# A hybrid attention and recurrence block on one core: where a recurrence head's keys and inputs are turned from feature-major to token-major

## The chip, the cores and the metric

The kernel runs on 1 core of one Trainium2 chip. The metric is the device time of one execution in microseconds (us), as the median of three runs. The engines are PE (TensorE; PEld is its weight loads), DVE (VectorE), ACT (ScalarE), POOL (GpSimd) and SP (SyncE, which only issues DMAs here).

## What is computed

The input x is 2048 x 1024 (f32). The block normalizes its rows, projects them with one matrix, and feeds two groups of heads: 8 attention heads over a sliding window of two chunks of 64 tokens, with a sink logit each, and 4 heads of a gated linear recurrence (HGRN2) of 128 features each. Both are gated with SiLU, joined, projected again, normalized and added to x. The recurrence is what the change touches, per head and chunk of 64 (the kernel works with chunks of 128, which it calls pairs):

```python
f = lb + (1 - lb) * sigmoid(f_logit); kk = 1 - f
G = cumsum(log(f))                      # inside a chunk
q_dec, k_dec = q * exp(G), kk * exp(-G)
A = tril(q_dec @ k_dec.T)
U = (kk * exp(G_last - G)).T @ v        # what the chunk adds to the state
state = exp(G_last) * state + U
o = A @ v + q_dec @ state_before
```

## The kernel before

The sequence is cut into 4 tiles of 512 tokens. All activations are kept with features on the partitions and tokens along the free dimension. A tile has 34 steps, one per block of weights: K (0), V (1), queries (2 to 5), attention gates (6 to 9), then four steps for each recurrence head h, `forget(h)`, `query(h)`, `value(h)` and `gate(h)` = 10 + 4h to 13 + 4h, and 8 steps of the output projection (26 to 33). In steps 0 to 25 PE runs 24 products L452 per step (8 slices of 128 features, each with high x high, low x high and high x low parts in FP32R); in the output steps it runs L461.

Everything else is placed into that stream by hand. `between` (L563) says ahead of which product of which step PE runs the small matmuls: `scores` and `turn` of the attention at product 4 of steps 8, 10, ..., 16, `weigh` at product 20, `head_scores(h)` at product 12 of step `gate(h)` (13, 17, 21, 25), `head_states(h)` at product 16 (head 0: 20) of the next step, `head_out(h)` at product 12 of step `gate(h) + 4` (head 3: product 16 of `gate(h) + 2`), `head_sum(h)` one step later. DVE and ACT each have one loop over tiles and steps (L1072 and L761), in which the order within a step is written out; the engines meet through counting semaphores.

A recurrence head goes like this. At `forget(h) + 1` DVE scales the logits out of PSUM (L1090), and ACT and DVE alternate through the logarithm of the gate and its cumulative sum (L1123 to L1160). At `query(h) + 1` DVE makes `k_mid` (L1137) and scales `f_d` (L1138). At `gate(h)`, which follows `value(h)`, DVE makes `q_mid` (L1108), `v_r`, the head's inputs (L1111), and `to_next` (L1112). `k_mid` and `v_r` are feature-major, but the state matmul (L540) and the output matmul (L549) need keys and inputs with tokens on the partitions. So `head_scores` waits for `k_mid` and `v_r` and turns both by 16 transposes on PE, each from 64 tokens' half of the partitions (L525), into the two banks of `score_b`; ACT copies them to `kv_tok` in one instruction (L810). Then PE computes the head's scores (L532). DVE masks them at the next step (`mask_head`, L1000). `head_states` waits for that mask and for `kv_tok`; `carry_head` (L1005 to L1020) chains the states on DVE.

`score_b` also holds the attention's scores (L481) and the sum of squares of a head's output (`head_sum`, L559), so PE waits in `head_scores` until DVE has read the attention's scores and ACT the previous sum, and in `scores` and ahead of the output steps until ACT has taken the turned keys.

Other work on the same queues at these steps: on DVE the softmax (`softmax_first` L1048 to L1057 at even steps from 8 to 14, `softmax_sums` L1062 to L1065 at odd steps from 9 to 15), the gating of the attention's output (L1129 at steps 11, 13, 15, 17), the gates' SiLU (L982, L986, L993 at step `gate(h) + 1`); in step 13 the order after `to_next` is softmax sums, then L1129, and PE's `turn` at step 14 (L493) waits for both. In tile 0 and the first six steps of tile 1, the weights are split into a high and a low part on the fly, ACT's L689 and then DVE's L906 at the end of nearly every step, for the block two or three steps on; SP saves them to memory, and later tiles load them ready-made. On ACT, the step `gate(h)` holds the eviction L810, then L689, then the squares of the previous head's output (L836, L837); POOL takes the low part of these (L1216) for `head_sum`.

## Time and profile before

| | before |
|---|---|
| median of 3 runs | 892.59 us (891.85 to 894.47) |
| profiled execution | 891.43 us |
| its span | 889.6 us |
| busy: PE, DVE, ACT, POOL | 877.8, 524.9, 422.1, 113.9 us |

The profiled execution lies 1.8 us above its span, which begins with the first instruction and ends with the last. A matmul's duration is its way through the array and overlaps its neighbours', so the pace of PE is read from the distance between starts. In a timeline row the columns are start, duration, engine, line, operation, output and input, shape and count; in brackets stands the idle time ahead of it and what ended that. A group `x8` of matmuls is merged into one row.

### The profile page before, as it was taken

What the parts mean: (1) busy time and instruction counts of PE and PEld (TensorE: products, weight loads), DVE (VectorE), ACT (ScalarE), POOL (GpSimd) and SP (SyncE); (2) the same over time, 40 slices, a digit from 0 to 9 for tenths busy, and PEclk for the clock granted to TensorE, in tenths of its full rate; (3) what the DMA queues carried; (4) which work ended last, traced back from release to release, by engine and by line L of the source; (5) the groups of instructions that cost most, each with busy time, mean ns of one, the idle gap of its engine ahead of it and who ended that gap; (6) DMA issues with size and microseconds to landing.
All of it is one profiled execution on the core that took longest, in us unless ns stands there. A gap on an engine that the chain in (4) does not pass through costs nothing.

```text
span 889.6 us, 12328 instructions
## 1 busy us (share of the span) xinstructions
PE 877.8 (99%) x4730; PEld 719.9 (81%) x4730; DVE 524.9 (59%) x848; ACT 422.1 (47%) x736; POOL 113.9 (13%) x90
## 2 busy tenths in 40 slices
PE   8999999999999999999999999999999999999997
PEld 6887788888888788888888877888888877788886
DVE  6778867763656764655153677465524367745523
ACT  7856456573654444445144534454523453445322
POOL 0000014420200001421020000242111000013012
PEclk9999999999999999999999999999999999999999
DMA  8686766629958543543785654345378544443463
GB/s 313 240 307 211 258 214 226 225 72 400 400 193 323 197 167 125 180 167 109 290 325 189 222 190 142 142 145 202 131 257 331 189 154 160 144 158 143 145 247 129
DMA packets 52922, 186.03 MB, mean 209 GB/s; under 512 B 5888, under 2 KB 6144, under 8 KB 52864
## 3 DMA queue, kind: packets, MB, share of 16 engines
q1 hardware_dynamic: 50128, 178.29, 56.3%
q10 hardware_dynamic: 2736, 6.95, 2.0%
q8 instruction: 38, 0.62, 0.3%
q14 instruction: 20, 0.16, 0.1%
HBM read 141.18 MB, written 44.04 MB: 208 GB/s over the span
## 4 chain that ended last, share of the span: by engine, by line
PE 95%; DVE 1%; ACT 1%; issue 1%; DMA 1%; SPq 0%; DVEq 0%; ACTq 0%
PE bank L452 62%; PE bank L461 10%; PE score_b L461 5%; PE turn_b L461 5%; PE bank L532 2%; PE turn_b L503 2%; PE score_b L481 2%; PE turn_b L549 2%; PE bank L540 2%; PE turn_b L552 2%; PE score_b L525 1%; PE turn_b L493 1%; DMA x_in<-in_x 1%; ACT w_hi L689 0%; PE score_b L560 0%
## 5 line engine op out<-in xcount | busy, mean ns | idle before, releaser
L452 PE MATMUL bank<-h_hi,w_hi 128*128 128x512 f32 x832 | 327.1, 394 | 1.3 <-ACT h_hi L726 1.3
L452 PE MATMUL bank<-h_hi,w_lo 128*128 128x512 f32 x832 | 327.5, 394 | 0.0
L452 PE MATMUL bank<-h_lo,w_hi 128*128 128x512 f32 x832 | 326.0, 392 | 0.0
L452 PEld LDWEIGHTS bank<-h_lo,w_hi 128*128 128x128 f32 x832 | 156.2, 188 | 36.4 <-issue 4.9
L452 PEld LDWEIGHTS bank<-h_hi,w_hi 128*128 128x128 f32 x832 | 156.4, 188 | 34.2 <-ACT h_hi L726 1.7
L452 PEld LDWEIGHTS bank<-h_hi,w_lo 128*128 128x128 f32 x832 | 156.3, 188 | 33.6 <-issue 1.0
L1216 POOL TENSOR_TENSOR mix_lo<-v_r,mix_hi 128x512 fp32r<-128x512 f32 x16 | 21.0, 1312 | 543.0 <-ACT v_r L837 543.0
L906 DVE TENSOR_TENSOR w_lo<-w_raw,w_hi 128x1024 fp32r<-128x1024 f32 x37 | 44.9, 1221 | 32.3 <-ACT w_hi L689 32.3
L810 ACT ACTIVATE kv_tok<-score_b 128x1024 f32<-128x1024 f32 x16 | 16.4, 1024 | 83.9 <-PE score_b L525 83.9
L461 PE MATMUL bank<-w_hi,mix_lo 128*128 128x512 f32 x128 | 50.5, 395 | 0.0
L689 ACT ACTIVATE w_hi<-w_raw 128x1024 fp32r<-128x1024 f32 x38 | 39.7, 1049 | 22.5 <-issue 10.0
L461 PE MATMUL bank<-w_hi,mix_hi 128*128 128x512 f32 x128 | 49.8, 389 | 0.0
L461 PE MATMUL bank<-w_lo,mix_hi 128*128 128x512 f32 x128 | 49.8, 389 | 0.0
L693 ACT ACTIVATE g_a<-g_b 128x512 f32<-128x512 f32 x32 | 20.2, 630 | 51.6 <-DVE g_b L982 51.5
L1200 POOL TENSOR_TENSOR x_acc<-x_acc,x_sq 128x512 f32<-128x512 f32 x21 | 32.9, 1564 | 60.2 <-ACT x_sq L722 60.1
L786 ACT ACTIVATE f_b<-bank 32x512 f32<-32x512 f32 x48 | 28.3, 589 | 25.6 <-PE bank L452 14.7
L986 DVE SCALAR_TENSOR_TENSOR g_a<-g_b,g_a 128x512 f32<-128x512 f32 x32 | 23.9, 748 | 27.8 <-ACT g_a L695 27.8
L982 DVE TENSOR_TENSOR g_b<-bank,x_scale 128x512 f32<-128x512 f32 x32 | 22.1, 689 | 26.4 <-PE bank L452 25.8
L704 ACT ACTIVATE g_a<-g_a 128x512 f32<-128x512 f32 x32 | 20.2, 632 | 36.0 <-DVE g_a L986 36.0
L1070 DVE TENSOR_TENSOR q_gate<-turn_b,w_post_t 128x512 f32<-128x512 f32 x8 | 5.5, 685 | 43.8 <-ACT f_c L733 43.8
L786 ACT ACTIVATE f_d<-bank 32x512 f32<-32x512 f32 x32 | 18.8, 589 | 22.7 <-PE bank L452 22.4
L795 ACT ACTIVATE probs_t<-turn_b 128x1024 f32<-128x1024 f32 x16 | 16.4, 1027 | 27.6 <-PE turn_b L493 27.5
(169 smaller groups left out, 1391.7 us busy)
## 6 DMA issues: line engine op xcount, KB each, us to landing
w_hi<-kept_hi SPq DMA_DIRECT2D x96, 512.0 KB, 3.8
w_lo<-kept_lo SPq DMA_DIRECT2D x96, 512.0 KB, 4.6
w_raw<-in_weights SPq DMA_DIRECT2D x38, 512.0 KB, 5.4
kept_hi<-w_hi SPq DMA_DIRECT2D x34, 512.0 KB, 5.9
kept_lo<-w_lo SPq DMA_DIRECT2D x34, 512.0 KB, 7.3
x_in<-in_x_rows SPq DMA_DIRECT2D x8, 1024.0 KB, 7.5
x_in<-in_x SPq DMA_DIRECT2D x15, 512.0 KB, 6.1
out<-q_gate ACTq DMA_DIRECT2D x9, 512.0 KB, 8.9
```

The source lines that it names most:

```text
L452: mm = pe.matmul(acc(w)[:, :], stationary[:, s, k, :], moving[:, k, :], start=(m == 0), stop=(m == 3 * KT - 1), skip_group_check=True)
L461: mm = pe.matmul(y_bank[half][b][:, :], mix[:, k, b * P:(b + 1) * P], weight[:, SPLIT_SLOT[t * WT + w], (k % 2) * 4:(k % 2) * 4 + 4, :].re ...
L481: mm = pe.matmul(score_b[:, g, pair(2 * odd + hp)], queries[half, hp, 2 * q + odd, :, :].rearrange("p j n -> p (j n)"), k_slots[half, q:q ...
L689: act.activation(w_hi[:, SPLIT_SLOT[i], :, :], w_raw[:, i % RAW_SLOTS, :, :], ACT.Copy).then_inc(hi_split.sem, 1)
L693: then(tile, act.activation(dst, src, ACT.Abs))
L704: act.activation(g_a[:, :], g_a[:, :], ACT.Exp).then_inc(gate_sig.sem, 1)
L786: copy = act.activation(dst[32 * b:32 * b + 32, :], acc(s - 1)[32 * (b ^ 1):32 * (b ^ 1) + 32, :], ACT.Copy)
L906: dve.tensor_tensor(w_lo[:, s, :, :], w_raw[:, i % RAW_SLOTS, :, :], w_hi[:, s, :, :], ALU.subtract).then_inc(lo_split.sem, 1)
L982: dve.tensor_tensor(g_b[:, :], acc(w)[:, :], x_scale[:, :], ALU.mult).then_inc(tile_read.sem, 1)
L986: dve.scalar_tensor_tensor(g_a[:, :], g_b[:, :], 0.0, g_a[:, :], ALU.min, ALU.subtract).then_inc(gate_arg.sem, 1)
L1200: pool.tensor_tensor(x_acc[:, :], x_acc[:, :], x_sq[:, :], ALU.add).then_inc(x_added.sem, 1)
L1216: pool.tensor_tensor(o_sq_lo, o_sq[:, :], o_sq_hi, ALU.subtract).then_inc(o_low.sem, 1)
```

## The change

Per head and in all four tiles (`DVE_TURN = 0`), PE's 16 transposes and ACT's eviction L810 are gone. DVE transposes `v_r` at step `gate(h)` with one 128 x 512 instruction, which turns each 32 x 32 square in its place, into `f_d` (`v_blocks`); ACT then puts the 16 squares of a pair where they belong with 16 copies, each of 32 partitions by 4 x 32 elements (`place_values`). The keys are turned by DVE alone, with 16 transposes of 32 partitions by 4 x 32 elements that write straight to the right partitions (`turn_keys`), queued after `to_next` and ahead of the softmax sums. Odd heads' inputs go to `v_spare`, the upper half of `probs`. The waits that guarded `score_b` for the transposes go from `head_scores`, `scores` and the output steps; `head_sum` gets two of them, and `head_states` waits for the keys' squares as well.

```diff
--- before.py
+++ after.py
@@ -119,6 +119,7 @@
 
 
 Y_POOL = (0, 2)
+DVE_TURN = 0
 
 
 FILL = {1: 1, 2: 2}
@@ -178,6 +179,7 @@
         probs_t = sb("probs_t", [8, P])
         v_win = sb("v_win", [CHUNKS, P])
         kv_tok = sb("kv_tok", [2, N])
+        v_spare = probs[:, PAIRS:, :].rearrange("p q n -> p (q n)")
         a_t = sb("a_t", [N])
         carry = sb("carry", [HEADS, P])
         read_state = sb("read_state", [PAIRS, P])
@@ -275,6 +277,7 @@
         mixa_lo, mixh_lo = count("mixa_lo", QT), count("mixh_lo", HEADS)
         x_added = count("x_added", KT - 1)
         y_scaled, finished_pool = count("y_scaled", 2), count("finished_pool", 2)
+        k_blocks, v_blocks = sem("k_blocks"), sem("v_blocks")
         pool_setup = sem("pool_setup")
 
         def loaded(sems, uses, tile, i, n=1):
@@ -310,6 +313,18 @@
                 engine.wait_ge(lo_split.sem, lo_split.after(tile, w))
             else:
                 engine.wait_ge(w_ready[slot], 32 * uses(slot, FRESH, i + 1))
+
+        def v_tok(t, h):
+
+            return v_spare if t >= DVE_TURN and h % 2 else kv_tok[:, 1, :]
+
+        def blocks_done(t, h):
+
+            return (t - DVE_TURN) * HEADS + h + 1
+
+        def square(ap, i, j):
+
+            return by_pair(ap)[32 * i:32 * i + 32, :, 32 * j:32 * j + 32]
 
         def state_pairs(t):
 
@@ -472,7 +487,7 @@
                 else:
                     pe.wait_ge(m_sub.sem, m_sub.after(t, q - 1))
                 for h in range(HEADS):
-                    if gate(h) + 1 == SCORES0 + 2 * q:
+                    if gate(h) + 1 == SCORES0 + 2 * q and t < DVE_TURN:
                         pe.wait_ge(kv_ready.sem, kv_ready.after(t, h))
                 for odd in range(2):
                     for hp in range(2):
@@ -512,10 +527,8 @@
                     mm = pe.transpose(value_b[:, pair(p)], v_t[:, pair(p)], ident)
                 mm.then_inc(values_turned.sem, 1)
 
-            def head_scores(t, h):
-
-                pe.wait_ge(k_mid_done.sem, k_mid_done.after(t, h))
-                pe.wait_ge(tile_read.sem, tile_read.after(t, value(h)))
+            def turn_head(t, h):
+
                 pe.wait_ge(m_sub.sem, m_sub.after(t, PAIRS - 1 if gate(h) >= SCORES0 + CHUNKS else (gate(h) - SCORES0) // 2))
                 pe.wait_ge(o_rstd.sem, o_rstd.after(t, h - 2))
                 for a, src in enumerate((k_mid, v_r)):
@@ -524,6 +537,13 @@
                             half = slice(64 * j, 64 * j + 64)
                             mm = pe.transpose(score_b[:, j, chunk(PAIRS * a + p)], src[half, pair(p)], ident[half, half])
                 mm.then_inc(kv_turned.sem, 1)
+
+            def head_scores(t, h):
+
+                pe.wait_ge(k_mid_done.sem, k_mid_done.after(t, h))
+                pe.wait_ge(tile_read.sem, tile_read.after(t, value(h)))
+                if t < DVE_TURN:
+                    turn_head(t, h)
                 if t + 1 < TILES or h == 0:
                     pe.wait_ge(carried.sem, carried.after(t, h - 1))
                 else:
@@ -535,9 +555,11 @@
             def head_states(t, h):
 
                 pe.wait_ge(kv_ready.sem, kv_ready.after(t, h))
+                if t >= DVE_TURN:
+                    pe.wait_ge(k_blocks, blocks_done(t, h))
                 pe.wait_ge(a_masked.sem, a_masked.after(t, h))
                 for p in range(state_pairs(t)):
-                    mm = pe.matmul(head_b[:, pair(p)], kv_tok[:, 0, pair(p)], kv_tok[:, 1, pair(p)], start=True, stop=True)
+                    mm = pe.matmul(head_b[:, pair(p)], kv_tok[:, 0, pair(p)], v_tok(t, h)[:, pair(p)], start=True, stop=True)
                 mm.then_inc(u_done.sem, 1)
 
             def head_out(t, h):
@@ -546,7 +568,7 @@
                 pe.wait_ge(o_gated.sem, o_gated.after(t, h - 1))
                 for p in range(PAIRS):
                     empty = t == 0 and p == 0
-                    mm = pe.matmul(out_b[:, pair(p)], kv_tok[:, 1, pair(p)], a_t[:, pair(p)],
+                    mm = pe.matmul(out_b[:, pair(p)], v_tok(t, h)[:, pair(p)], a_t[:, pair(p)],
                                    start=True, stop=empty, skip_group_check=True)
                     if not empty:
                         mm = pe.matmul(out_b[:, pair(p)], read_state[:, p, :], q_mid[h % 2][:, pair(p)],
@@ -556,6 +578,9 @@
             def head_sum(t, h):
 
                 pe.wait_ge(o_low.sem, o_low.after(t, h))
+                if t >= DVE_TURN:
+                    pe.wait_ge(m_sub.sem, m_sub.after(t, PAIRS - 1))
+                    pe.wait_ge(o_rstd.sem, o_rstd.after(t, h - 1))
                 pe.matmul(score_b[:, 1, :], ones_r[:, :], o_sq_hi, start=True, stop=False, skip_group_check=True)
                 pe.matmul(score_b[:, 1, :], ones_r[:, :], o_sq_lo, start=False, stop=True,
                           skip_group_check=True).then_inc(o_summed.sem, 1)
@@ -626,7 +651,8 @@
 
 
                 pe.wait_ge(mixa_lo.sem, mixa_lo.after(t, QT - 1))
-                pe.wait_ge(kv_ready.sem, kv_ready.after(t, HEADS - 1))
+                if t < DVE_TURN:
+                    pe.wait_ge(kv_ready.sem, kv_ready.after(t, HEADS - 1))
                 order = [(2 * w + i, b) for w in range(3) for b in range(4) for i in range(2)] + [(KT - 2, b) for b in range(4)]
                 step = 3 * (KT - 1)
                 for i, (k, b) in enumerate(order):
@@ -707,6 +733,14 @@
                 act.wait_ge(m_sub.sem, m_sub.after(t, q))
                 act.activation(sink_d[:, :], sink_d[:, :], ACT.Exp, scale=SCALE)
                 act.activation(probs[:, :, :], probs[:, :, :], ACT.Exp, scale=SCALE).then_inc(p_exp.sem, 1)
+
+            def place_values(t, h):
+                act.wait_ge(v_blocks, blocks_done(t, h))
+                act.wait_ge(o_done.sem, o_done.after(t, h - 2))
+                for i in range(4):
+                    for j in range(4):
+                        copy = act.activation(square(v_tok(t, h), j, i), square(f_d[:, :], i, j), ACT.Copy)
+                copy.then_inc(kv_ready.sem, 1)
 
             def rstd(tile, src, dst, width, bias=eps[:, :]):
 
@@ -806,6 +840,9 @@
 
                     for head in range(HEADS):
                         if s == gate(head):
+                            if t >= DVE_TURN:
+                                place_values(t, head)
+                                continue
                             act.wait_ge(kv_turned.sem, kv_turned.after(t, head))
                             act.activation(kv_tok[:, :, :].rearrange("p a (b j n) -> p j (a b) n", j=2, n=CHUNK),
                                            score_b[:, :, :].rearrange("p j (b n) -> p j b n", n=CHUNK), ACT.Copy).then_inc(kv_ready.sem, 1)
@@ -1018,6 +1055,15 @@
                         then(t, follows)
                 if t + 1 < TILES:
                     dve.tensor_scalar(carry[:, h, :], pair_state[:, PAIRS - 1, :], to_end[:, h % 2, PAIRS - 1:], None, ALU.mult).then_inc(carried.sem, 1)
+
+            def turn_keys(t, h):
+
+                dve.wait_ge(k_mid_done.sem, k_mid_done.after(t, h))
+                dve.wait_ge(u_done.sem, u_done.after(t, h - 1))
+                for i in range(4):
+                    for j in range(4):
+                        last = dve.transpose(square(kv_tok[:, 0, :], j, i), square(k_mid[:, :], i, j))
+                last.then_inc(k_blocks, 1)
 
             def gate_head(t, h):
 
@@ -1109,7 +1155,12 @@
                         dve.wait_ge(head_mixed.sem, head_mixed.after(t, h_of - 2))
                         dve.wait_ge(tile_done.sem, tile_done.after(t, value(h_of)))
                         dve.tensor_tensor(v_r[:, :], acc(value(h_of))[:, :], x_scale[:, :], ALU.mult).then_inc(tile_read.sem, 1)
+                        if t >= DVE_TURN:
+                            dve.wait_ge(tile_read.sem, tile_read.after(t, value(h_of)))
+                            dve.transpose(f_d[:, :], v_r[:, :]).then_inc(v_blocks, 1)
                         then(t, dve.tensor_tensor(to_next[:, :], to_end[:, h_of % 2, 0:PAIRS - 1], to_mid[:, h_of % 2, 1:], ALU.mult))
+                        if t >= DVE_TURN:
+                            turn_keys(t, h_of)
                     for k in H_PARTS.get(s, ()) if t + 1 < TILES else ():
                         low_h(t + 1, k)
                     if not odd and 0 <= q < PAIRS:
```

## Rows read from the trace of the kernel before

**Rows 1.** The page, part 1: busy time of each engine
```profile
PE 877.8 (99%) x4730; PEld 719.9 (81%) x4730; DVE 524.9 (59%) x848; ACT 422.1 (47%) x736; POOL 113.9 (13%) x90
```

**Rows 2.** The page, part 4: the chain, shares by engine and by line
```profile
PE 95%; DVE 1%; ACT 1%; issue 1%; DMA 1%; SPq 0%; DVEq 0%; ACTq 0%
PE bank L452 62%; PE bank L461 10%; PE score_b L461 5%; PE turn_b L461 5%; PE bank L532 2%; PE turn_b L503 2%; PE score_b L481 2%; PE turn_b L549 2%; PE bank L540 2%; PE turn_b L552 2%; PE score_b L525 1%; PE turn_b L493 1%; DMA x_in<-in_x 1%; ACT w_hi L689 0%; PE score_b L560 0%
```

**Rows 3.** Windows, tiles 0 and 1: start:end, length, busy us (instructions), clock, DMA
```profile
90.00:100.00 10.00, 9.85 (x85) 8.03 (x84) 9.08 (x16) 3.09 (x4) 0.00 (x0) 1.00 0.89 279
...
340.00:350.00 10.00, 10.00 (x70) 8.67 (x70) 2.41 (x6) 4.42 (x7) 2.55 (x2) 1.00 0.39 134
```

**Rows 4.** Timeline of PE, tile 1, second head: start us, us, engine, line, operation
```profile
342.30 0.39 PE L552 MATMUL turn_b<-q_even,read_state 128*128 128x128 f32 x2
...
343.26 1.16 PE L532 MATMUL bank<-v_t,k_mid 128*128 128x128 f32 x8
```

**Rows 5.** Timeline of DVE, tile 1, step 13
```profile
308.63 0.69 DVE L1111 TENSOR_TENSOR v_r<-bank,x_scale 128x512 f32<-128x512 f32 x1 [0.68 <-PE bank L452]
309.24 0.15 DVE L1112 TENSOR_TENSOR to_next<-to_end,to_mid 128x3 f32<-128x3 f32 x1
312.26 0.68 DVE L1129 TENSOR_TENSOR q_gate<-turn_b,q_gate 128x512 f32<-128x512 f32 x1
```

**Rows 6.** Timeline of DVE: small multiplications of carry_head, tile 0
```profile
116.15 0.28 DVE L1014 TENSOR_SCALAR read_state<-probs,to_next 128x128 f32<-128x128 f32 x1
116.35 0.34 DVE L1012 SCALAR_TENSOR_TENSOR probs<-probs,to_next,bank 128x128 f32<-128x128 f32 x1
```

**Rows 7.** Timeline of ACT, tile 0: a tiny, a 512-element and a weight instruction
```profile
85.04 0.19 ACT L802 ACTIVATE to_end<-f_c 128x4 f32<-128x4 f32 x1
85.14 0.62 ACT L803 ACTIVATE f_d<-f_c 128x512 f32<-128x512 f32 x1
85.66 1.04 ACT L689 ACTIVATE w_hi<-w_raw 128x1024 fp32r<-128x1024 f32 x1
```

**Rows 8.** Timeline of PE, tile 1, step 14
```profile
317.57 0.66 PE L493 MATMUL turn_b<-sq_in,probs 64*128 64x64 f32 x16
```

**Rows 9.** Timeline of DVE, tile 0, steps 13 to 25
```profile
94.65 0.68 DVE L1129 TENSOR_TENSOR q_gate<-turn_b,q_gate 128x512 f32<-128x512 f32 x1
...
98.40 1.23 DVE L1048 TENSOR_REDUCE s_stats<-score_b 128x8 f32<-128x1024 f32 x1 [0.72 <-PE score_b L481]
...
101.78 0.69 DVE L986 SCALAR_TENSOR_TENSOR g_a<-g_b,g_a 128x512 f32<-128x512 f32 x1 [0.62 <-ACT g_a L695]
...
105.78 0.69 DVE L1090 TENSOR_TENSOR f_b<-bank,x_scale 128x512 f32<-128x512 f32 x1 [0.43 <-PE bank L452]
...
120.39 0.68 DVE L1111 TENSOR_TENSOR v_r<-bank,x_scale 128x512 f32<-128x512 f32 x1
...
125.76 1.23 DVE L906 TENSOR_TENSOR w_lo<-w_raw,w_hi 128x1024 fp32r<-128x1024 f32 x1 [3.55 <-ACT w_hi L689]
...
134.38 0.69 DVE L1090 TENSOR_TENSOR f_b<-bank,x_scale 128x512 f32<-128x512 f32 x1 [0.52 <-PE bank L452]
...
149.42 0.68 DVE L1111 TENSOR_TENSOR v_r<-bank,x_scale 128x512 f32<-128x512 f32 x1
...
153.03 1.23 DVE L906 TENSOR_TENSOR w_lo<-w_raw,w_hi 128x1024 fp32r<-128x1024 f32 x1 [1.76 <-ACT w_hi L689]
...
161.61 0.69 DVE L1090 TENSOR_TENSOR f_b<-bank,x_scale 128x512 f32<-128x512 f32 x1
...
176.66 0.68 DVE L1111 TENSOR_TENSOR v_r<-bank,x_scale 128x512 f32<-128x512 f32 x1
```

**Rows 10.** Timeline of PE, tile 0, steps 14 and 21
```profile
98.19 0.66 PE L493 MATMUL turn_b<-sq_in,probs 64*128 64x64 f32 x16
...
150.20 0.47 PE L525 MATMUL score_b<-sq_in,k_mid 64*128 64x64 f32 x8 [0.70 <-issue]
150.85 1.16 PE L532 MATMUL bank<-q_even,k_mid 128*128 128x128 f32 x8
```

## The prediction

> **What bounds the kernel now.** I read the page's busy line first: PE is busy for 99% of the span, with DVE at 59% and ACT at 47% [rows 1]. Then the chain that ended last: 95% of it is PE, and 1% of it is L525, the 16 transposes of each head that the change removes [rows 2]. So the kernel runs at the pace of PE's queue, and whatever leaves that queue shortens it one for one, provided that nothing else then arrives late. Hence the third view, the windows. The average of 59% hides two kinds of stretch. Around the first head of tile 0 DVE works for 9.08 of 10 us and PE already misses 0.15 us of the window; around the second head of tile 1 it works for 2.41 of 10 us [rows 3]. The clock is 1.00 in both, so no part of the sum is a matter of clock. In tile 0 DVE also rounds off the weights (L906 in nearly every step), which later tiles load ready-made.
>
> The question is therefore: what does PE save per head, and where does the work put on DVE and ACT make PE wait instead?
>
> **What leaves PE.** A full matmul takes 0.22 us of the queue: L452 has 62% of the 889.6 us [rows 2] and by the code 4 x 26 x 24 = 2,496 products. In tile 1 the last matmul ahead of a head's transposes starts at 342.30, so the next one could start at 342.52; after the 16 transposes L532 starts at 343.26 [rows 4]. The block costs 0.74 us. With 4 tiles of 4 heads that is at most 16 x 0.74 = 11.8 us. ACT's eviction L810 goes as well, 16 times; PE never waited for it in the chain, so this alone gives nothing.
>
> **What comes onto DVE.** Per head one 128x512 transpose (f_d) and 16 of 32 partitions by 128 elements (keys). The trace has no DVE transpose. The large one is priced like v_r's multiplication, whose successor starts 0.61 us after it [rows 5]. For the small ones the lower bound is the multiplication L1014 on 128 elements, which lasts 0.28 us but lets the next start after 0.20; the upper is the full 0.34 us of L1012 with no overlap [rows 6]. I take 0.225 us, nearer the lower, because like L1014 they have one input and no dependence on each other: 16 x 0.225 = 3.6 us (3.2 to 5.4). With about 0.1 us for the wait on v_r's own semaphore, DVE reaches its next job D = 0.6 + 0.1 + 3.6 = 4.3 us later in each head.
>
> Against this change speaks the Trainium skill, "VectorE: DVE Perf Modes", section "Rules for kernel authors": a 128x128 transpose belongs on TensorE if a PSUM destination is acceptable, since DVE only turns 32 by 32 blocks. The same page gives 311 ns for 128x128 elements in bf16; end to end 16 of those would be an estimated 5.0 us instead of 3.6, and the sum below would come out some 7 us later (1.4 in each of four first heads and 0.8 in two more heads of tile 0). No run here shows a DVE transpose; this hangs together with the first rival.
>
> **What comes onto ACT.** 16 copies of 32 x 128. ACT's smallest instruction (L802, 4 elements) lasts 0.19 us but the next starts after 0.10; L803 with 512 elements lasts 0.62 [rows 7]. Elements thus cost (0.62 - 0.19)/508 = 0.85 ns each, so 128 last 0.30 us and, overlapped by 0.10, take 0.20 of queue: 16 x 0.20 = 3.2 us (bounds 1.6, at L802's pace, and 4.8, without overlap). ACT no longer waits for PE, since it starts once f_d is there.
>
> **Tiles 1 to 3, first head.** This is the step (13) in which DVE must still normalize a softmax and gate an output before PE's next transposes L493. v_r starts at 308.63, and the gating L1129 runs from 312.26 to 312.94 [rows 5]. With D it ends at 317.25, and PE may go on at about 317.3. PE wanted L493 at 317.57 [rows 8], now at 317.57 - 0.74 = 316.83. It waits 0.5 us. Three tiles: 1.5 us (none at 3.2 us for the keys, 2.3 us each at 5.4). Queued behind the same turn are L999, L1000 and L982: the state matmuls need the mask L1000 only 16 products later, the bank freed by L982 is wanted three steps later, and DVE's idle time before the next softmax absorbs the delay. **The other nine heads of these tiles** cost nothing: DVE then stands idle until PE delivers the scores (2.41 of 10 us busy [rows 3]); if that cover were gone, each would lose what D exceeds the idle time by.
>
> **Tile 0, first head.** The gating L1129 runs from 94.65 to 95.33 [rows 9]; with D it ends at 99.63. PE's L493 started at 98.19 [rows 10] and now starts at 99.7: PE is 1.5 us *behind* the old kernel here, its saving included. DVE stays late; the gaps that it can give up until L1090 are 0.72, 0.62 and 0.43 us (at 98.40, 101.78 and 105.78), which with the overlap that an idle start loses make 1.9. So the second head's f chain starts 2.4 us late, and v_r, at 120.39 before, comes at 122.8. PE meets it in time: it has a head's output matmuls in front. Its saving brings PE to 1.5 - 0.7 = 0.8 us behind.
>
> **Tile 0, third and fourth head.** Here the old kernel already has PE waiting for v_r: 0.70 us before L525 at 150.20 [rows 10], and the fourth head has the same pattern. head_scores keeps that wait. From here I follow DVE and ACT. After v_r of the second head, L906 came at 125.76, after an idle 3.55 us for ACT's w_hi [rows 9]. Now ACT must first wait for f_d (0.8 us after v_r ends), copy for 3.2, then make w_hi (L689, 1.05, [rows 7] shows one behind L803): 5.1 us after v_r's end, where L906 came 4.7 us after it (125.76 - 121.07); some 0.5 us more, which the idle 0.52 at 134.38 swallows. So the third head's v_r comes 2.4 us late, at 149.42 + 2.4 = 151.8, ends at 152.5, and L532 starts at 152.6 instead of 150.85: PE is 1.75 behind. Next head: L906 came 2.9 us after v_r's end (153.03 - 150.10), now 5.2: 2.3 more, with hardly any idle time before L1090 at 161.61 to absorb it. v_r of the fourth head, at 176.66 before, is 4.6 us late. Before, L532 followed v_r's end by 0.74 (150.85 - 150.11); now by 0.07. PE is 4.6 - 0.7 = 3.9 us behind. After the fourth head DVE has idle time again, and nothing more is lost.
>
> **Order and queues.** No DMA is moved. SP's load of w_raw waits on w_lo, so in tile 0 it shifts with L906, against a cover of two to three steps per weight block. POOL's square correction stands behind ACT's squares, which stand behind the 16 copies; in tiles 1 to 3 the copies begin earlier than the old eviction did, and PE's sum comes 16 products into the following step. The two added waits of head_sum are for events several steps old: nothing.
>
> **Sum.** Tiles 1 to 3: -12 x 0.74 + 1.5 = -7.4. Tile 0: +3.9. Together -3.5 us. The profiled execution took 891.43 us (span 889.6) and would take 887.9. The median of the runs is 892.59, 1.2 above it, so I put the time at **889.1 us**. 0.3%, or 2.7 us, is about what a measurement of this kernel can tell from no change.
>
> **Rivals.**
> 1. *DVE becomes the bound in step 13 and tile 0* (slower). Place: L1129 before L493, and v_r before L532. Price at the upper bounds (5.4 for keys, 4.8 for ACT): tiles 1 to 3 wait 1.8 more each (5.4); in tile 0 the first head passes on 1.8 more, and each of the next two 1.6 (ACT's copies): 5.0. The sum is -3.5 + 10.4 = +6.9, or 899.5. It turns from gain to loss when the small transposes take about 0.28 us each (0.9 more per head, in the first heads of four tiles), and is over 0.3% slower from about 0.32. For it: 91% busy DVE in tile 0. Against: independent small instructions overlap in these rows. The skill's rule above would make it come true.
> 2. *The cost is a little higher than I take it and nearly cancels the saving* (0.25 to 0.28 us each): about 890.5 to 893, no change. For it: my sum is the difference of terms of 8.9, 1.5 and 3.9.
> 3. *Everything is hidden*: small transposes at L1014's pace and ACT at 1.6 us. Then 892.6 - 11.8 = 880.8. Against: PE waits for v_r in tile 0 already, and with the waits that remain 885 is nearer.
> 4. *PE saves nothing*, because the 0.74 us are a change-over that L532 would pay anyway: then tiles 1 to 3 stay as they are (L1129 would be done before 317.57) and tile 0 loses its 3.9: 896.5. Against: between the ordinary products and the 128-row matmuls L552 there is no such gap.
>
> **Numbers.** Forecast with its near surroundings, 885 to 889.9, 0.42 (faster by over 0.3%), full saving 0.07, rival 2 0.30 (same), rivals 1 and 4 together 0.21 (slower). Faster 0.49, same 0.30, slower 0.21. The range reaches from rival 3 with the waits that remain, 884, to most of rival 1, 897.
>
> **What would show it.** Right: in tiles 1 to 3, L532 follows the products with no gap; L493 of step 14 waits for DVE by about half a microsecond; DVE's busy time rises by some 16 x 5 us; in tile 0 PE waits before L493 (2.5 us) and before L532 in the third and fourth heads (about 2 and 3 us). Wrong: a small transpose beyond 0.28 us of queue, ACT copies beyond 0.3, or a wait at head_states for the mask or the copies, which I hold to be covered by about a microsecond in tile 0.

## The result, and the profile after

The changed kernel takes **905.39 us**, median of 4 runs (904.96 to 907.99), against 893.0 for the kernel before beside it (891.85 to 894.47): a ratio of 1.0147, with a 95% interval of 1.0135 to 1.0158. It is slower by 1.5%, and the time lies above the predicted range. The profiled execution took 904.96 us; the rows below are its own. Rows of the page of the changed kernel, against [rows 1, 2]:

```profile
span 903.2 us, 12340 instructions
...
PE 874.3 (97%) x4474; PEld 714.4 (79%) x4474; DVE 606.4 (67%) x1120; ACT 487.3 (54%) x976; POOL 115.9 (13%) x90
...
PE 63%; DVE 16%; ACT 11%; issue 7%; POOL 1%; DMA 1%; SPq 0%; DVEq 0%; ACTq 0%; POOLq 0%
...
L1065 DVE STREAM_TRANSPOSE kv_tok<-k_mid 32x128 f32<-32x128 f32 x256 | 77.5, 303 | 3.8
...
L742 ACT ACTIVATE probs<-f_d 32x128 f32<-32x128 f32 x128 | 39.6, 310 | 33.3 <-DVE f_d L1160 31.9
L742 ACT ACTIVATE kv_tok<-f_d 32x128 f32<-32x128 f32 x128 | 39.6, 309 | 25.4 <-DVE f_d L1160 24.0
```

PE has 256 instructions fewer, but its busy time fell by 3.5 us only (877.8 to 874.3) while the span grew by 13.6: PE now waits. The chain, 95% PE before, holds 16% of DVE and 11% of ACT. What PE waits for, from the waits of PE of the changed kernel (us in total, times, longest):

```profile
PE turn_b L508 <- DVE q_gate L1180: 9.2, 4, 3.5
PE score_b L584 <- POOL mix_lo L1267: 4.1, 6, 1.8
PE bank L552 <- issue: 3.9, 2, 1.9
PE bank L618 <- DVE ones_r L945: 3.1, 1, 3.1
PE turn_b L571 <- DVE read_state L1051: 1.5, 2, 1.0
```

Two shorter waits, of 1.0 and 0.4 us, are left out. L508 is the old L493 (the first transposes of step 14), L552 the old L532 (its waits marked "issue" end with v_r: in the third head of tile 0 v_r ends at 157.19 and L552 starts at 157.29), L584 `head_sum`, L571 the first matmul of `head_out`. L618 is outside the change: every execution read here has those 3.1 us. The step that answers to [rows 5], in the timeline of DVE, tile 1 of the changed kernel:

```profile
322.77 0.69 DVE L1157 TENSOR_TENSOR v_r<-bank,x_scale 128x512 f32<-128x512 f32 x1 [0.68 <-PE bank L467]
323.49 0.71 DVE L1160 STREAM_TRANSPOSE f_d<-v_r 128x512 f32<-128x512 f32 x1
...
324.29 5.05 DVE L1065 STREAM_TRANSPOSE kv_tok<-k_mid 32x128 f32<-32x128 f32 x16
329.36 1.22 DVE L1108 TENSOR_REDUCE s_stats<-probs 128x8 f32<-128x1024 f32 x1
...
332.20 0.68 DVE L1180 TENSOR_TENSOR q_gate<-turn_b,q_gate 128x512 f32<-128x512 f32 x1
```

The 16 key transposes hold DVE for 5.05 us, 0.316 from one start to the next where each lasts 0.303: no overlap at all. v_r to gating was 3.63 us [rows 5] and is 9.43 (332.20 - 322.77). In the same step, the timeline of PE of the changed kernel, against [rows 8]:

```profile
325.25 1.05 PE L552 MATMUL bank<-q_even,k_mid 128*128 128x128 f32 x8
...
329.87 1.16 PE L496 MATMUL score_b<-k_t,q_gate 64*128 64x128 f32 x16
332.94 0.71 PE L508 MATMUL turn_b<-sq_in,probs 64*128 64x64 f32 x16 [1.90 <-DVE q_gate L1180]
```

Here PE stands still for 1.90 us. To see where the 13.6 us went I took, for each step of a head, the start of the same PE instruction in both traces; the table shows by how many us it is later than before (the sign - is earlier), and what came just ahead (a wait, or a clock below 1.00). The column e1 is the same shift for an experiment told below; the notes are the changed kernel's:

```
start before, step                  after   e1 (own start +1.40 taken off)
 86.69 tile 0, end of step 12       +0.09    0.0
 92.46 scores of head 0             -0.59   -0.65
 98.19 transposes of step 14        +3.06   -0.66    wait 3.49 for the gating L1180
102.64 PV product, same step        +5.41   -0.65    clock 0.50
131.46 states of head 1             +5.06   +1.03
147.78 output of head 1             +5.74   +1.71
158.69 states of head 2             +8.53   +4.49    wait 1.9 for v_r; clock 0.50 to 0.75
185.89 states of head 3            +12.51   +8.42    wait 1.9 for v_r, 1.83 for POOL L1267
191.56 output of head 3            +14.14   +8.42    clock 0.51 to 0.64
274.66 tile 1 begins               +14.13  +10.23
316.58 tile 1, L481 of step 14     +13.29   +9.37
317.57 transposes of step 14       +15.37   +9.38    wait 1.90 for the gating L1180
396.57 scores of head 3            +12.98   +6.95
404.38 states of head 3            +14.03   +7.92    wait 0.83 for POOL L1267
493.33 tile 2 begins               +14.04   +7.94
712.00 tile 3 begins               +13.92   +5.64
846.60 output of the last head     +13.52   +3.08
```

So tile 0 lost 14.1 us, and tiles 1 to 3 gained together 0.6 where 7.4 was forecast. The saving itself is there at every head: -0.74 at L552, another -0.10 at the products after it (tile 1, second head: 14.67 to 14.57). What eats it in tiles 1 to 3 is 2.08 us in each first head, and 1.1 in the last heads of tiles 1 and 2 (0.4 and 0.5 in the last two of tile 3), of a kind that I had not foreseen. Timelines of ACT and PE of the changed kernel, last head of tile 1:

```profile
410.17 5.13 ACT L742 ACTIVATE probs<-f_d 32x128 f32<-32x128 f32 x16 [3.44 <-DVE f_d L1160]
415.33 0.60 ACT L873 ACTIVATE mix_hi<-turn_b 128x512 fp32r<-128x512 f32 x1
415.82 0.60 ACT L874 ACTIVATE v_r<-turn_b 128x512 f32<-128x512 f32 x1
```

```profile
417.83 0.50 PE L584 MATMUL score_b<-mix_hi,ones_r 128*128 128x512 f32 x1 [0.83 <-POOL mix_lo L1267]
```

The squares of the head before stand behind the 16 copies on ACT, POOL's correction behind the squares, and PE's sum behind that. In tile 0 the long wait also brings something else. The windows of the changed kernel there (start:end, length, busy us and instructions of PE, PEld, DVE, ACT, POOL, then the granted clock, DMA share, GB/s):

```profile
96.00:98.00 2.00, 1.76 (x19) 1.17 (x18) 1.90 (x7) 1.92 (x7) 0.00 (x0) 1.00 0.47 184
98.00:100.00 2.00, 0.00 (x0) 0.00 (x0) 1.90 (x4) 0.76 (x1) 0.00 (x0) 0.90 0.01 2
100.00:102.00 2.00, 0.75 (x14) 0.75 (x16) 2.00 (x3) 0.00 (x0) 0.00 (x0) 0.50 0.02 4
102.00:104.00 2.00, 2.00 (x12) 1.59 (x9) 2.00 (x4) 1.45 (x2) 0.00 (x0) 0.50 0.25 53
104.00:106.00 2.00, 2.00 (x6) 1.52 (x6) 1.93 (x4) 1.47 (x3) 0.00 (x0) 0.50 0.92 281
106.00:108.00 2.00, 2.00 (x9) 1.39 (x7) 1.30 (x3) 1.16 (x2) 0.00 (x0) 0.90 1.02 418
```

PE idles through 98 to 100, and from 100 to 106 it works at 0.50, the lower of its two levels (1.2 instead of 2.4 GHz): the stretch 104 to 106 holds 6 of its instructions, where 106 to 108, mostly at full clock, holds 9. Between L508 and the PV product it loses 2.35 us to that, without any wait. It happens three times in tile 0: 2.35 us here, 1.88 of the 2.09 lost before the states of head 2 (0.21 is a wait for POOL), and 1.63 before the output of head 3. That is 5.9 us of the 14.1.

### The profile page after: what moved, and what is told of

It reads as the page before. It is cut to its first block, busy times and chain, and to the rows that moved or that the text cites. A ratio compares the mean times of both kernels' runs of the same rounds, so it can differ in the third digit from the quotient of the medians.

```text
span 903.2 us, 12340 instructions
## 1 busy us (share of the span) xinstructions
PE 874.3 (97%) x4474; PEld 714.4 (79%) x4474; DVE 606.4 (67%) x1120; ACT 487.3 (54%) x976; POOL 115.9 (13%) x90
## 4 chain that ended last, share of the span: by engine, by line
PE 63%; DVE 16%; ACT 11%; issue 7%; POOL 1%; DMA 1%; SPq 0%; DVEq 0%; ACTq 0%; POOLq 0%
PE bank L467 37%; PE bank L476 9%; PE turn_b L476 5%; PE score_b L476 4%; DVE kv_tok L1065 2%; ACT kv_tok L742 2%; DVE f_a L1199 1%; PE turn_b L518 1%; DVE f_c L1209 1%; PE bank L562 1%; PE score_b L496 1%; ACT probs L742 1%; ACT w_hi L715 1%; DVE g_a L1023 1%; DVE s_stats L1108 1%
## 5 line engine op out<-in xcount | busy, mean ns | idle before, releaser
L1065 DVE STREAM_TRANSPOSE kv_tok<-k_mid 32x128 f32<-32x128 f32 x256 | 77.5, 303 | 3.8
L742 ACT ACTIVATE probs<-f_d 32x128 f32<-32x128 f32 x128 | 39.6, 310 | 33.3 <-DVE f_d L1160 31.9
L742 ACT ACTIVATE kv_tok<-f_d 32x128 f32<-32x128 f32 x128 | 39.6, 309 | 25.4 <-DVE f_d L1160 24.0
```

Of the source, the lines that this page charges most:

```text
L742: copy = act.activation(square(v_tok(t, h), j, i), square(f_d[:, :], i, j), ACT.Copy)
L1065: last = dve.transpose(square(kv_tok[:, 0, :], j, i), square(k_mid[:, :], i, j))
```

## Experiments

Theory A: the 16 small instructions on each engine cost 0.316 and 0.320 us apiece, and so DVE bounds the first head and DVE and ACT together the later heads of tile 0. The expectations of e1 to e3 set two others against it. Theory B: the new waits and their order cost the time, whatever the instructions take. Theory C: the main cost is ACT's copies, with w_hi and the squares behind them. Two more questions came up on the way: whether a long wait is paid twice, in the wait and in the clock after it (called the double price below), and what makes a small instruction slow, the turning as such, a write to other partitions, or the short form. What is said "by PE's starts" is counted as in the table; the beginning of the program, before any head, varies by 0 to 3.5 us between executions and is taken off there, but not in the medians.

**e1, e2, e3: one instruction in place of 16.** In `turn_keys` (e1), in `place_values` (e2), and in both (e3):

```diff
-                for i in range(4):
-                    for j in range(4):
-                        last = dve.transpose(square(kv_tok[:, 0, :], j, i), square(k_mid[:, :], i, j))
+                last = dve.transpose(kv_tok[:, 0, :], k_mid[:, :])
...
-                for i in range(4):
-                    for j in range(4):
-                        copy = act.activation(square(v_tok(t, h), j, i), square(f_d[:, :], i, j), ACT.Copy)
+                copy = act.activation(v_tok(t, h), f_d[:, :], ACT.Copy)
```

> The changed kernel, but the keys are turned by one 128x512 transpose on DVE instead of 16 of 32x128 (squares stay in place: the turned keys are not moved to their partitions, so that part of the computation is left out). Theory A, the number of small DVE instructions is what costs (16 took 5.05 us of queue): DVE is about 4.4 us earlier per head, the waits before L508 (9.2 us) and the slow clock after the first of them (about 2.4) vanish, ACT's 16 copies still delay tile 0's third and fourth heads: 905.4 - 11.7 and a little more, 889 to 894. Theory B, the new waits and their order cost the time, whatever the instructions take: 903 to 906. Theory C, the ACT copies behind which w_hi and the squares stand are the main cost: 900 to 904.

> The changed kernel, but ACT places the inputs with one 128x512 copy instead of 16 of 32x128 (the squares are not moved to their partitions, that part is left out). Theory A: the waits before L508 stay; in tile 0 w_hi comes earlier but DVE's keys end only 0.7 us sooner than the copies did, and the waits for POOL's low part of the squares (4.1 us) vanish: 905.4 - 6, 897 to 901. Theory B: 903 to 906. Theory C: 890 to 894.

> Both of the above: one transpose for the keys and one copy for the inputs (neither moved to their partitions, left out). If PE's saving of 0.74 us per head is real and everything else is hidden once the small instructions are gone, 893.0 - 11.8 = 881, or up to 883 with what remains in tile 0. If the transposes' 0.74 us were a change-over that PE pays anyway, 892 to 893. Theory B: 903 to 906.

Measured: e1 895.44 (ratio 1.0019, 1.0009 to 1.0029); e2 904.6 (1.0119, 1.0103 to 1.0136); e3 **879.19** (0.9841, 0.9827 to 0.9856). e1 lies just above the range of theory A (889 to 894), and e3 below the 881 to 883 expected of it. e2 misses A's range (897 to 901) and falls into B's (903 to 906); e8 below shows why. B expected 903 to 906 of e3 as well, and C 890 to 894 of e2, so e3 rules out the first and e2 the second. The three parts do not add. Against the changed kernel, short keys alone give 10.0 us, short copies alone 0.8, both 26.2. The parts run side by side: DVE turns the keys while ACT copies. In e1 step 14 is free (third column of the table: -0.66 at 98.19, -0.65 at 102.64), the waits for the gating are 0.5 us in all instead of 9.2, but from the states of head 1 on tile 0 still loses: 8.4 us up to its last head and 1.8 in the steps behind it, because ACT's copies alone delay the next w_hi, w_lo and v_r. Two falls of the clock (1.9 and 1.6 us) are in it. In e2 the keys alone do so (tile 0 +11.3), and the gating waits stay at 9.2. With both short, tile 0 gains 2.8 and the whole run, by PE's starts, 12.9 (from +0.54 to -12.38), against 16 x 0.84 = 13.4 for the full saving: the 16 v_r transposes of 0.71 us and the new waits cost next to nothing. The loss is the price of 32 small instructions per head.

**e4: tile 0 left as it was.**

```diff
-DVE_TURN = 0
+DVE_TURN = 1
```

> The changed way only from tile 1 on, tile 0 as before (DVE_TURN = 1). The events of PE put 14.1 us of the loss into tile 0 and a net gain of 0.1 to 0.6 us into the three others together: theory A expects 892.4 to 893.2, the same as before within what can be told. If the loss of tile 0 was only handed on from a general slowing (clock, contention), a loss of 3 us or more stays: 896 or more.

Measured: 893.19, median of 10 (890.25 to 896.38), ratio 1.0004 (0.9989 to 1.002). The loss of tile 0 is away (12.2 us); tiles 1 to 3 alone gain 0.55 by PE's starts, no difference that can be told. The runs scatter over 6 us; the two longest (896.1 and 896.4) have a mean granted clock of 0.994, the two shortest (890.3 and 890.4) 0.999; e8 bears on that.

**e5: the first head's keys behind the gating of step 13**, from tile 1 on. Nobody needs them before the states, 16 products later.

```diff
-                        if t >= DVE_TURN:
+                        if t >= DVE_TURN and h_of:
                             turn_keys(t, h_of)
...
+                    if kind == 2 and h_of == 0 and t >= DVE_TURN:
+                        turn_keys(t, 0)
```

> As the version that starts at tile 1, and the first head's 16 key transposes stand behind the softmax sums and the gating of step 13 on DVE instead of ahead of them. Theory A: the 2.08 us by which PE's L508 slipped in each of three tiles turn into nothing: 893.2 - 6.2 = 887. Theory B (the waits themselves) or a wait that takes this one's place (the mask or the keys before the state matmuls in step 14, now later on DVE by 1 us): 890 to 893.

Measured: 887.0, ratio 0.9939 (0.9924 to 0.9953). The waits for the gating (5.7 us in e4) are gone from PE's list, and 6.2 us of the median with them. It is the order in DVE's queue that cost the time, not DVE's load: the same 16 instructions run in the same step. By PE's starts tiles 1 to 3 now gain 7.2 us.

**e7: the same move with tile 0 changed as well.**

> As e5_keys_late, but in tile 0 too (DVE_TURN = 0). The long wait of 3.5 us before tile 0's first L508 and the slow clock behind it go (6 us), but DVE and ACT owe the same work before the second to fourth heads: theory A expects 905.4 - 6.2 - 4 to 6 = 893 to 896. If the wait before L508 was the whole cause of tile 0's loss, 886 to 888.

Measured: 899.06, ratio 1.007 (1.0053 to 1.0087), above the 893 to 896 expected. Tile 0 still loses 12.3 us of its 14.1: a wait of 2.8 us for the gating L1180, which the forecast did not have, now stands ahead of the next softmax's L508 (112.04 before), with a clock of 0.50 at 116 to 122 behind it that costs 2.9 us more. Around the first head of tile 0 DVE has hardly any idle time to which the keys could be moved (9.08 of 10 us busy, [rows 3]); so I put this part of the loss down to load and not to order. That is argued: no other order was tried in tile 0.

**e8: the suspected wait made longer.** e4 with 8 more key transposes ahead of the first head's 16.

```diff
+                if h == 0:
+                    for i in range(2):
+                        for j in range(4):
+                            last = dve.transpose(square(kv_tok[:, 0, :], j, i), square(k_mid[:, :], i, j))
+                    last.then_inc(k_extra, 1)
+                    dve.wait_ge(k_extra, t)
```

> As the version that starts at tile 1, with 8 more key transposes ahead of the first head's 16, so that PE waits some 4.5 us instead of 1.9 before L508 in three tiles. If PE only waits, 893.2 + 3 x 2.6 = 901. If the granted clock falls to half after so long a wait, as it did in tile 0 of the changed kernel, 2.3 to 2.6 us more in each: 908 to 909.

Measured: 907.61, ratio 1.0172 (1.0157 to 1.0187), 14.4 us above e4. The waits grew from 1.9 to 4.5 us, three times 2.6 = 7.8, and the rest is in the windows of e8, tile 1 (columns as above):

```profile
320.00:322.00 2.00, 0.38 (x8) 0.18 (x4) 1.93 (x5) 0.00 (x0) 0.00 (x0) 1.00 0.98 381
322.00:324.00 2.00, 0.00 (x0) 0.00 (x0) 1.90 (x4) 0.00 (x0) 0.00 (x0) 0.56 0.19 78
324.00:326.00 2.00, 1.17 (x17) 1.06 (x17) 2.00 (x5) 0.01 (x1) 0.00 (x0) 0.50 0.00 0
326.00:328.00 2.00, 2.00 (x5) 1.61 (x6) 1.93 (x5) 1.94 (x3) 0.00 (x0) 0.50 0.00 0
328.00:330.00 2.00, 2.00 (x8) 1.53 (x8) 1.56 (x2) 1.21 (x3) 0.00 (x0) 0.73 0.00 0
```

Behind each of the three waits PE loses another 1.9, 1.4 and 2.75 us between the transposes and the PV product, 6.0 in all. The double price is real, beside theory A: a wait of 4.5 us costs some 6.5. (908 to 909 was expected.) The changed kernel's own waits of 1.90 us in tile 1 brought no fall, while waits of the same length in e2 did. The changed kernel, and then e2, in the same step of tile 1:

```profile
332.00:334.00 2.00, 1.06 (x18) 0.96 (x19) 2.00 (x5) 0.31 (x1) 0.00 (x0) 1.00 0.55 215
334.00:336.00 2.00, 2.00 (x11) 1.64 (x10) 1.93 (x5) 1.94 (x3) 0.00 (x0) 1.00 0.00 0
```

```profile
331.00:333.00 2.00, 1.13 (x18) 1.02 (x19) 2.00 (x5) 0.37 (x1) 0.00 (x0) 1.00 0.47 193
333.00:335.00 2.00, 2.00 (x7) 1.58 (x6) 1.93 (x5) 1.94 (x4) 0.00 (x0) 0.51 0.00 0
335.00:337.00 2.00, 2.00 (x7) 1.55 (x7) 1.51 (x2) 0.95 (x2) 0.00 (x0) 0.63 0.00 0
```

e2 lost 1.65, 1.6 and 1.5 us that way in tiles 1 to 3, 4.8 in all; without them it would have come to about 900, inside theory A's range. That is most of why e2 is hardly faster than the changed kernel although its copies are short. It would fit the scatter of e4, whose waits are as long; but e4's profiled execution has three waits of 1.9 us and no fall, and its longest ones have no trace. What decides between the two outcomes was not found.

**e6 and e9: the last head's sum.** On top of e5, the squares of the head before go ahead of the 16 copies on ACT: for every head (e6), or for the last alone (e9). The core of e9; in e6 the condition is `if h:`

```diff
             def place_values(t, h):
                 act.wait_ge(v_blocks, blocks_done(t, h))
+                if h == HEADS - 1:
+                    square_out(t, h - 1)
                 act.wait_ge(o_done.sem, o_done.after(t, h - 2))
...
-                        if s == out_step(head):
+                        if s == out_step(head) and (head != HEADS - 2 or t < DVE_TURN):
```

> As e5_keys_late, and on ACT the squares of the previous head's output stand ahead of the 16 copies instead of behind them. Theory A: the slips of 1.05, 1.06 and 0.3 us before the last head's state matmuls vanish as well: 2.4 us less than e5_keys_late, about 884.5, which would be 12 x 0.74 = 8.9 below the kernel before. If the copies, now some 2 us later, reach the state matmuls too late, no gain or a loss against e5.

> As e5_keys_late, with the squares ahead of the copies on ACT for the last head alone, the one whose state matmuls PE reached too early. In e6 the copies of the other heads, moved back, made ACT and then v_r late, and PE waited 0.6 us before the last head's scores in each of tiles 1 and 2. If that is so, this version keeps the gain of e5 and adds 1.0, 1.0 and 0.3 us: 884.5 to 885.5. If the last head's wait is a matter of anything else, 887 as e5.

Measured: e6 885.54 (0.9926, 0.9907 to 0.9946), no more than e5 within the intervals. The waits of L584 are gone, but in the other heads the squares delay ACT's further work: v_r of the last head starts at 395.80, in e5 at 394.59 (0.3 us of this is e6's later beginning), and PE waits 0.60 us for it in tiles 1 and 2. e9 leaves those heads alone: **882.29**, median of 5 (881.4 to 884.99), ratio **0.9888** (0.987 to 0.9906). It does the whole work of the reference and beats both kernels, by 1.1% and 2.6%. Its page, against [rows 1, 2]:

```profile
span 880.0 us, 12340 instructions
...
PE 868.0 (99%) x4538; PEld 712.5 (81%) x4538; DVE 586.8 (67%) x1052; ACT 469.5 (53%) x916; POOL 115.4 (13%) x90
...
PE 92%; DVE 3%; ACT 2%; issue 1%; DMA 1%; SPq 0%; POOL 0%; DVEq 0%; ACTq 0%
```

and all that PE waits for in e9:

```profile
PE bank L618 <- DVE ones_r L950: 3.1, 1, 3.1
PE bank L467 <- ACT h_hi L767: 1.4, 2, 0.9
PE score_b L538 <- issue: 1.4, 2, 0.7
PE turn_b L518 <- ACT probs_t L836: 0.4, 1, 0.4
```

DVE's busy share (67%) is that of the changed kernel, and PE is at 99% again. L538 is the old L525, still in tile 0, with the v_r wait of [rows 10]. By PE's starts tiles 1 to 3 gain 9.65 us (+0.05 to -9.60); 12 x 0.84 would be 10.1. In e5 they gain 7.2 and in e6 8.4, so the new order is worth 2.5 us over e5, as forecast. The medians of e5 and e9 differ by 4.7, and e9 lies below the 884.5 to 885.5 expected; in the profiled executions the other 2.2 us come from the beginning (+2.2 in e5, +0.05 in e9).

**e10 and e11: why is a small instruction so long?** Both on top of e5. e10 puts a plain copy in place of each key transpose, so the turning is left out; e11 takes the squares along diagonals on both engines, so that instructions next to each other read and write different partitions.

```diff
-                        last = dve.transpose(square(kv_tok[:, 0, :], j, i), square(k_mid[:, :], i, j))
+                        last = dve.tensor_copy(square(kv_tok[:, 0, :], j, i), square(k_mid[:, :], i, j))
```

```diff
-                        last = dve.transpose(square(kv_tok[:, 0, :], j, i), square(k_mid[:, :], i, j))
+                        a, b = j, (i + j) % 4
+                        last = dve.transpose(square(kv_tok[:, 0, :], b, a), square(k_mid[:, :], a, b))
```

> As e5_keys_late, with the 16 key transposes replaced by 16 copies of the same form (32x128, other partitions, DVE); the keys are not turned inside their squares, so this leaves the turning out. If it is the transpose that lets nothing overlap, the copies' starts lie 0.20 to 0.22 us apart; if it is the form (32 partitions, four runs of 32 elements, one partition group after the other), they lie 0.28 or more apart.

> As e5_keys_late, with the 16 squares of keys and of inputs taken along diagonals, so that no two neighbouring instructions read or write the same group of 32 partitions. If instructions queue because they share a partition group, the starts come closer than the 0.316 and 0.320 us of the changed kernel (0.22 to 0.25); if each small instruction is simply run to its end, nothing moves and the time is that of e5, 887.

Measured: e10 886.92 (0.9932, 0.9913 to 0.9952), e11 886.0 (0.9922, 0.9903 to 0.9941); neither differs from e5, so in that order the keys' price is hidden, as it should be. A row of e10's page:

```profile
L1065 DVE COPY kv_tok<-k_mid 32x128 f32<-32x128 f32 x192 | 44.0, 229 | 2.7
```

A copy lasts 218 ns at the median (229 mean) with starts 0.23 us apart, between the 0.20 to 0.22 and the 0.28 or more of the two expectations; the turning adds about 85 ns. The copies do not overlap either. In e11 a transpose still lasts 303 ns and an ACT copy 308, so instructions do not queue because they share partitions. Nor is it the write to other partitions: of the 16 transposes of a head, the four with i = j write to the partitions that they read, and they take 0.30 us like the rest. Even at e10's 0.23 us DVE would be 3.7 us later per head, so the number of instructions is the larger part of the price.

One rival is left. In the order of the kernel every small instruction writes to another group of 32 partitions than the one before, and in e11 it reads another as well; no version keeps two neighbours on one group. Yet the first key transpose, which reads and writes the first group, stands in e5 right behind the gating, whose 128 partitions begin there too. Timeline of DVE of e5, tile 1:

```profile
315.15 0.68 DVE L1180 TENSOR_TENSOR q_gate<-turn_b,q_gate 128x512 f32<-128x512 f32 x1
315.75 5.04 DVE L1065 STREAM_TRANSPOSE kv_tok<-k_mid 32x128 f32<-32x128 f32 x16
```

It starts 0.08 us before the gating ends, and so in all three tiles. A short form alone does not forbid overlap, then; the change of group from one instruction to the next may be what does. That is not shown, and for ACT there is no such pair.

## Why the prediction was wrong

**What failed first: the 0.225 us for a small transpose.** I took it "nearer the lower, because like L1014 they have one input and no dependence on each other". The kernel starts one every 0.316 us, near the upper end of 0.34, and past the 0.28 at which I had said that gain turns into loss. D came out at 5.8 us instead of 4.3 (v_r to gating, 3.63 before and 9.43 after). Each first head of tiles 1 to 3 lost 2.08 us instead of 0.5: 4.7 of the 17.1 us between forecast and trace (+13.6 against -3.5). Tile 0 makes 10.2 more, the chain through POOL in tiles 1 to 3 3.1, and 1.2 are in favour (below): 16.8.

**The ACT copies, 0.20 us taken, bounds 0.10 to 0.30**, came out at 0.320: above both ends. The elements' price was right (0.30 us for 128 elements, measured 0.309); the overlap was not. A row of the kernel before was nearer in kind than L802 and L803: four instructions of 32 partitions in a row, each on another group, in the timeline of ACT at the start.

```profile
22.01 2.39 ACT L786 ACTIVATE f_b<-bank 32x512 f32<-32x512 f32 x4
```

0.60 us each, with no overlap. A sum with "no overlap" on both engines (5.4 and 4.8) was my rival 1.

**"The other nine heads of these tiles cost nothing"** was argued for DVE alone. ACT's queue had squares, and through POOL a sum of PE, behind the copies; I had named this chain and held that the copies "begin earlier than the old eviction did", which does not help when they last 5.13 us instead of one eviction. It took 3.1 us in tiles 1 to 3, mostly in the last heads, and up to 1.83 in tile 0. e9 takes it away.

**"No part of the sum is a matter of clock."** I read the clock of the kernel before and took it for a constant. The change makes waits, and behind three of them the clock fell: 5.9 us in tile 0, none in the forecast.

**Tile 0: +3.9 forecast, +14.1 measured.** First head +3.06 instead of +1.5 (D), clock 5.9; the v_r waits of the third and fourth heads came where predicted (1.9 us each, seen at L552 as "issue"; predicted about 2 and 3), and the sum's chain through POOL came on top. So did two waits of L571 for `read_state` (0.5 and 1.0 us), which DVE computes late in `carry_head`; the forecast had no such term.

**What was right.** The block costs PE 0.74 us in each of the 12 heads of tiles 1 to 3 (0.68 in the first of tile 0); with the product after it it was even 0.84, 1.2 us in favour. v_r's transpose: successor after 0.63, taken 0.6. The wait on v_r's own semaphore: 0.72 from v_r's start to the transpose, 0.11 above the usual 0.61, taken 0.1. DVE's busy time rose by 81.5 us, forecast 80. The places of the waits, L508 and L552, and their releasers. Rival 4 is refuted by e3. Rival 1, at 899.5 (0.21 together with rival 4), named the right mechanism and the right turning point; the time is 5.9 above its figure. Its key price was close (5.4 against 5.05), and it had no clock and no sum chain, so part of that nearness is luck. Two figures of the prediction don't agree with the rest of it: in rival 4, where PE saves nothing, tile 0 would lose the full 4.6 by which v_r is late, and the time would be 897.2 instead of 896.5; and rival 3 with the waits that remain is put at 885 in one place and at 884 in another.

The rows show 303 ns for a DVE transpose of 32 x 128 f32 elements, and 16 of them in 5.05 us. The rule of the Trainium skill cited in the prediction ("VectorE: DVE Perf Modes", section "Rules for kernel authors": such turns belong on TensorE) pointed to the right side, and the estimate made from that page's figure, 5.0 us per head, agrees with the trace, 5.05, though that figure is for bf16 and not for this form. In e9, where the keys stand behind the gating, the rule does not decide: PE gains what DVE pays, since DVE's time there is free.

## What to carry to other kernels

Price a run of small instructions by count times full duration, from rows of the same form and the same change of partitions, until a row shows overlap: 16 of 32 x 128 took 5 us on either engine, where one of 128 x 512 took 0.7. Before moving work to an engine that is "67% busy", walk each queue from the place where it lands to the next thing that the bounding engine waits for; here a move of 16 instructions behind one gating, and of two squares ahead of the copies, turned no gain (e4) into 1.1% (e9). And count a new wait of PE of about 2 us or more with the slower clock that may follow it.

## What the runs showed of the hardware

- Instructions on 32 partitions whose group of partitions changed from one to the next did not overlap on DVE (transposes 0.303 long, 0.316 apart; copies 0.218 and 0.23) or on ACT (0.309 and 0.320), where instructions on 128 partitions in the same queues do (L1014: 0.28 long, next after 0.20 [rows 6]; L873: 0.60 and 0.49). Behind the gating, which begins on the same group, a 32-partition transpose did overlap, by 0.08 us (e5).
- A DVE transpose of 128 x 512 f32 lasted 0.71 us, one of 32 x 128 0.303: an estimate of 1.06 ns per element of a partition (0.407/384) and 0.17 us for the instruction, if the number of partitions costs nothing. No run separates the two for a transpose; on ACT 32 x 512 lasted 0.59 us and 128 x 512 0.60 to 0.62.
- The granted clock fell to 0.50, for 3.4 to 6.8 us, during or within 1.5 us behind all six waits of PE of 2.8 us or more (3.5 in the changed kernel and in e2, 2.8 in e7, three of 4.5 in e8), and behind 9 of 20 waits of 1.8 to 1.95 us (two of six in the changed kernel, both in e1, all five in e2, none of the seven in e4 and e7). Each fall cost 1.4 to 2.9 us.
